# RWKV stage of a hybrid decoder step: transposes that accumulate for the sample states, row groups side by side, rank 160 cut as 80 and 80

## The chip, the cores and the metric

The kernel runs on one core of a Trainium2 chip. The metric is device time of one execution in microseconds; for the kernel before, three runs gave 1702.85, 1702.91 and 1709.01, so the median is 1702.91. One execution was profiled, and its span from first to last instruction is 1701.4 us.

## The reference

One inference step of four layers (gated DeltaNet, mLSTM, RWKV-7, gated DeltaNet), each followed by a squared-ReLU MLP, on a prompt of 256 tokens and 8 samples of one token, all sharing weights. D = 1024, so the activations are 1024 x 264 (256 + 8 columns). Everything is float32. Of the RWKV-7 layer what matters here is:

```python
xr, xw, xk, xv, xa, xg = (h + xx * mu[j] for j in range(6))
r, k, v = xr @ w_rkv[0], xk @ w_rkv[1], xv @ w_rkv[2]
w_log = -softplus(-(w0 + tanh(xw @ w1) @ w2)) - 0.5          # w1: 1024x64, w2: 64x1024
a = sigmoid(a0 + (xa @ a1) @ a2)                             # rank 64
g = sigmoid(xg @ g1) @ g2                                    # rank 160
# per sample, 16 heads of 64x64: one step of the state
s = s * w_t[:, :, None, :] + sa[..., None] * b_t[:, :, None, :] + v_t[..., None] * k_t[:, :, None, :]
```

## The kernel before, in words

Every engine has a program of its own, written by hand in order; semaphores (`wait_ge`, `then_inc`) tie them together. TensorE (PE) writes the eight banks of PSUM (`ps[0]` to `ps[7]`); ScalarE (ACT) or VectorE (DVE) copies a bank out, and `last_read[b]` holds the semaphore value that says bank b is free. A weight stream of 1 MB units goes through a ring of five slots, loaded by SyncE. A product of float32 operands that are not marked as split appears in the trace as two MATMUL records; the transposes of line 747 (`tp`, identity as the moving operand) and the split products of the MLPs appear as one each. In this document "logical" products are those written in the code.

The RWKV layer runs on PE in this order (`rwkv`, from line 1431):

1. Keys: 64 logical products `w_rkv[1]` x `xk`, k outermost (lines 1437 to 1445), all eight banks. The mixed inputs sit in two buffers: `xj[0]` holds xk, then xa, then xr; `xj[1]` holds xw, then xg, then xv. DVE (`mixed`, line 3041) may fill `xj[0]` with xa when all key products are done (line 3060), and the later ones on `lo_mm` (line 3062).
2. Down-projections (lines 1455 to 1468): four groups of 8 logical products, of 64 (w1), 64 (a1), 128 and 32 (the 160 of g1) stationary columns, into banks 3, 4, 5, 6. Then eight small transposes of the shifted row into banks 0 and 1.
3. Up-projections (`back`, line 1479): eight tiles of w2 from partitions 0 to 63 and `lo[0]`, then eight of a2 from partitions 0 to 63 and `lo[1]`. ACT takes each tile out with a sigmoid (lines 2237 to 2240).
4. `decays_to_rows` (line 1496): 16 transposes into banks 0 to 3, at once after the up-projections; then the 64 products of r with hooks between its tiles, the first of which is `cumulate_decays`; then the 64 of v.
5. Gate up-projection (line 1581 and 1632): per tile one product over 128 rows and one over 32 rows, four tiles, then four `gram` groups of 64 x 64 products, then four tiles.
6. `invert64` (line 860) inverts 64 x 64 triangular blocks in six levels. Each level has the steps (l, 0), (l, 1) and, from level 1, (l, 2), (l, 3). `PLACES` (line 554) names the steps after which a fill runs, two parts each: parts 0 to 7 are `sample_update`, 8 to 31 are `gram` and `token_major`. Sample updates sat at (0, 0), (0, 1), (1, 0), (1, 1).
7. `sample_update(q)` (line 1606) makes the new states of head pair q in bank 6 or 7: four logical products of the state (stationary, 128 x 128, already scaled by GpSimd) with the identity, which transpose it and add it in PSUM, then one product over 32 rows and 512 columns that adds the two outer products. ACT copies the bank to `rS` (line 2307), SyncE stores it.

Of the kernel before, what the change touches and what calls it, by code (L numbers as in the profile page):

```python
# [12 lines left out]
P = 128  # L13
D = 1024
# [77 lines left out]
def hybrid_trunk(nc, a, o):  # L92
# [11 lines left out]
    with ctx:  # L104
# [237 lines left out]
        rg_mm = semaphore("rg_mm")  # L342
        shT_mm = semaphore("shT_mm")
# [210 lines left out]
        PLACES = [(0, 0), (0, 1)] + [(l, i) for l in range(1, LEVELS64) for i in range(4)][:14]  # L554
# [183 lines left out]
        def _(pe):  # L738
# [692 lines left out]
            def rwkv(j):  # L1431
# [5 lines left out]
                for k in range(KT):  # L1437
                    pe.wait_ge(xj_ok, count.seen(xj_ok))
                    for t in range(KT):
# [16 lines left out]
                for i in range(4):  # L1456
                    if i == 2:
                        w = unit_in()
                    cut = (slice(0, 64), slice(64, 128), slice(0, 128), slice(128, 160))[i]
                    b = 3 + i  # L1460
                    pe.wait_ge(*last_read[b])
                    for k in range(KT):
                        if i < 3:
# [29 lines left out]
                back([(64, 0, lo[0])], w)  # L1493
                back([(64, D, lo[1])], w)

                def decays_to_rows():
                    pe.wait_ge(rk_ev, 2 * KT)
# [61 lines left out]
                def sample_reads(q0):  # L1559
# [9 lines left out]
                    if q0 == NP - 2:  # L1569
# [11 lines left out]
                back([(P, 0, lo[2]), (32, D, lo[3])], w, range(4))  # L1581
# [24 lines left out]
                def sample_update(q):  # L1606
                    b = 6 + q % 2
                    if q == 0:
                        pe.wait_ge(mvb_ok, count.seen(mvb_ok))
                        pe.wait_ge(ct_ev, count.seen(ct_ev, 2))  # L1610
                    if q % 2 == 0:
                        pe.wait_ge(qs_ok, count.seen(qs_ok))
                    pe.wait_ge(*last_read[b])
                    r_ = slice(32 * (q % 4), 32 * (q % 4) + 32)
                    for m in range(4):
                        mm(ps[b][:, m * P:(m + 1) * P], rST[:, q, m, :], ident[:], m == 0, False)
                    mm(ps[b][:], RT[r_, 1, q // 4, :], MV[q // 4][r_].rearrange("p s k -> p (s k)"), False, True).then_inc(
                        rt_mm, count.up(rt_mm))
                    last_read[b] = su_ev, count.expect(su_ev)
# [12 lines left out]
                back([(P, 0, lo[2]), (32, D, lo[3])], w, range(4, KT))  # L1632
# [3 lines left out]
                def first_fill(n):  # L1636
                    b = 6 + n % 2
                    if n < 8:
                        sample_update(n)
                    elif n < 12:  # L1640
# [198 lines left out]
        def _(ac):  # L1839
# [380 lines left out]
            def rwkv(j):  # L2220
# [9 lines left out]
                for i, (n, f) in enumerate(((64, ACT.Tanh), (64, ACT.Copy), (P, ACT.Sigmoid), (32, ACT.Sigmoid))):  # L2230
# [1358 lines left out]
```

## Time and profile before

| what | value |
|---|---|
| median of three runs | 1702.91 us |
| span of the profiled execution | 1701.4 us |
| PE busy | 1648.5 us, 97% of the span |
| DVE, ACT, POOL busy | 1029.4, 839.2, 240.6 us |
| mean granted TensorE clock | 0.994 |
| RWKV stretch that the change touches | about 767 to 985 us |

The profiled execution has no time of its own beside its span. The median of the runs is 1.5 us above the span. A timeline row gives the start, the length of the group from first start to last end, the engine, line, operation, operands, partitions x columns of the stationary operand, the form of the moving one and the count; the ends of matmuls are modelled, so the pace of a group is read from its start to the next group's start.

### The profile page before, as it was taken

Reading aid. Unit: us, or ns where it says so; the run is one execution under the profiler, and the core shown is the slowest. Engines: PE = TensorE matmul, PEld = TensorE weight load, DVE = VectorE, ACT = ScalarE, POOL = GpSimd, SP = SyncE. Lnnn points to the kernel's source line nnn. Section 1 sums busy time; section 2 is a strip of 40 time slices with the busy share of each in tenths; the row PEclk is TensorE's granted clock in tenths of the full one; section 3 lists DMA queues with packets and bytes.
Section 4 is the critical chain, followed back from the end, with each engine's and each line's share of the span. In section 5 each row is a group of like instructions: output and inputs, shape, how many; then the busy total and the mean of one; then the engine's idle time right before and its main releaser. Section 6 shows DMA issues by size and latency. Waiting matters only on the chain.

```text
span 1701.4 us, 40128 instructions
## 1 busy us (share of the span) xinstructions
PE 1648.5 (97%) x17533; PEld 1554.2 (91%) x17533; DVE 1029.4 (61%) x1688; ACT 839.2 (49%) x1599; POOL 240.6 (14%) x293
## 2 busy tenths in 40 slices
PE   7999999999998999999999999999999999999997
PEld 6999899999896999997786987999998998899997
DVE  6965677744557776435361355777448946777654
ACT  5754566633545665331522214666336745566533
POOL 6005340000010200011003130200000016310000
PEclk9999999999999999999999999999999999999999
DMA  7941345556653656544323001555557531465650
GB/s 213 273 148 38 114 146 176 190 180 199 205 160 110 213 189 197 182 138 123 127 90 112 16 4 33 147 180 188 183 174 229 175 100 40 120 195 178 198 174 26
DMA packets 244963, 250.27 MB, mean 147 GB/s; under 512 B 15936, under 2 KB 238686, under 8 KB 244702
## 3 DMA queue, kind: packets, MB, share of 16 engines
q1 hardware_dynamic: 237040, 224.74, 42.0%
q0 software_dynamic: 7440, 22.86, 4.6%
q8 instruction: 139, 2.28, 0.6%
q14 instruction: 36, 0.29, 0.1%
q10 hardware_dynamic: 308, 0.10, 0.0%
HBM read 229.75 MB, written 18.32 MB: 146 GB/s over the span
## 4 chain that ended last, share of the span: by engine, by line
PE 91%; DVE 5%; ACT 3%; issue 1%; DMA 0%; SPq 0%; DVEq 0%
PE ps L743 89%; PE ps L747 2%; DVE tri L2434 1%; DVE hn L2442 1%; ACT acts L1843 1%; DVE acts L2442 0%; DVE mixer_lo L2434 0%; ACT hn L1843 0%; DVE acts L2434 0%; DVE st L2442 0%; DVE st L2434 0%; DMA acts<-in_x_sample_dram 0%; ACT w_mlstm L1843 0%; ACT w_gdn L1843 0%; DVE acts L2438 0%
## 5 line engine op out<-in xcount | busy, mean ns | idle before, releaser
L2434 DVE TENSOR_TENSOR w_mlp<-ring,w_mlp 128x1024 fp32r<-128x1024 f32 x256 | 311.7, 1224 | 121.6 <-ACT w_mlp L1843 115.6
L1843 ACT ACTIVATE w_mlp<-ring 128x1024 fp32r<-128x1024 f32 x256 | 269.4, 1054 | 211.6 <-PE ps L743 211.6
L743 PE MATMUL ps<-hn_split,w_mlp 128*128 128x264 f32 x3072 | 373.3, 284 | 0.0
L743 PE MATMUL ps<-h_split,w_mlp 128*128 128x264 f32 x3072 | 372.6, 284 | 0.0
L743 PEld LDWEIGHTS ps<-hn_split,w_mlp 128*128 128x128 f32 x3072 | 372.0, 188 | 0.3
L743 PEld LDWEIGHTS ps<-h_split,w_mlp 128*128 128x128 f32 x3072 | 371.6, 188 | 0.0
L743 PE MATMUL ps<-gdn_hi,w_gdn 128*128 128x264 f32 x1024 | 194.9, 289 | 7.2 <-DVE mixer_lo L2434 7.0
L1843 ACT ACTIVATE tri<-ps 128x264 f32<-128x264 f32 (+4 forms) x184 | 80.9, 442 | 212.2 <-PE ps L743 211.5
L743 PEld LDWEIGHTS ps<-gdn_hi,w_gdn 128*128 128x128 f32 x1024 | 162.6, 190 | 10.8 <-issue 8.9
L1843 ACT ACTIVATE acts<-ps 128x264 f32<-128x264 f32 (+4 forms) x126 | 56.3, 451 | 205.9 <-PE ps L743 204.3
L743 PE MATMUL ps<-mixer_lo,w_gdn 128*128 128x264 f32 x512 | 146.7, 286 | 0.0
L743 PE MATMUL ps<-tri 64*64 64x64 f32 x3602 | 126.3, 221 | 3.1 <-DVE tri L2434 2.7
L743 PEld LDWEIGHTS ps<-tri 64*64 64x64 f32 x3602 | 113.3, 135 | 14.3 <-issue 12.1
L2434 DVE TENSOR_TENSOR tri<-tri 128x264 f32<-128x264 f32 (+4 forms) x145 | 59.9, 413 | 101.4 <-ACT h_split L1843 100.6
L743 PE MATMUL ps<-acts,ring 128*128 128x264 f32 (+2 forms) x448 | 105.5, 396 | 3.3 <-DVE acts L2442 2.8
L743 PEld LDWEIGHTS ps<-acts,ring 128*128 128x128 f32 (+2 forms) x448 | 83.2, 188 | 22.2 <-issue 4.9
L743 PEld LDWEIGHTS ps<-mixer_lo,w_gdn 128*128 128x128 f32 x512 | 98.1, 192 | 0.0
L2434 DVE TENSOR_TENSOR tri<-tri,ps 128x512 f32<-128x512 f32 (+1 forms) x88 | 52.5, 636 | 71.6 <-PE ps L743 71.4
L2434 DVE TENSOR_TENSOR w_gdn<-ring,w_gdn 128x1024 fp32r<-128x1024 f32 x64 | 77.9, 1218 | 21.3 <-ACT w_gdn L1843 21.3
L3444 POOL TENSOR_TENSOR hn<-hn 128x264 f32<-128x264 f32 x15 | 12.0, 797 | 510.8 <-ACT hn L1843 509.1
L2442 DVE SCALAR_TENSOR_TENSOR acts<-ps,cw,acts 128x253 f32<-128x253 f32 x144 | 69.3, 481 | 14.8 <-ACT acts L1843 11.1
L743 PE MATMUL ps<-mlstm_hi,w_mlstm 128*128 128x264 f32 x384 | 75.0, 292 | 3.1 <-DVE mixer_lo L2434 3.1
(406 smaller groups left out, 2329.3 us busy)
## 6 DMA issues: line engine op xcount, KB each, us to landing
ring<-in_ffn_w_dram SPq DMA_DIRECT2D x128, 1024.0 KB, 5.4
ring<-in_gdn_w_in_dram SPq DMA_DIRECT2D x32, 1024.0 KB, 6.2
ring<-in_ml_w_in_dram SPq DMA_DIRECT2D x12, 1024.0 KB, 5.3
ring<-in_rw_w_rkv_dram SPq DMA_DIRECT2D x12, 1024.0 KB, 5.1
st<-in_state_gdn_S_dram POOLq DMA_DIRECT2D x2, 4096.0 KB, 24.0
ring<-in_gdn_w_out_dram SPq DMA_DIRECT2D x8, 1024.0 KB, 5.0
out_gdn_S_s_dram<-st SPq DMA_DIRECT2D x16, 512.0 KB, 3.9
st<-in_state_mlstm_C_dram POOLq DMA_DIRECT2D x1, 4096.0 KB, 19.7
```

The costliest lines, as they stand in the source:

```text
L743: return nc.tensor.matmul(out, lhsT, rhs, start=start, stop=stop)
L747: return nc.tensor.transpose(out, in_, ident[0:n, 0:n])
L1843: return nc.scalar.activation(out, in_, f, bias=bias, scale=scale)
L2434: return nc.vector.tensor_tensor(out, in0, in1, op)
L2442: return nc.vector.scalar_tensor_tensor(out=out, in0=in0, scalar=s, in1=in1, op0=op0, op1=op1)
L3444: last = gp_.tensor_tensor(sq[:, 0, :], sq[:, 0, :], sq[:, k, :], ALU.add)
```

## The change

Five things are changed.

- The products of w1 and a1 now alternate: for each k one product into partitions 0 to 63 of bank 3 from `xj[1]` and one into partitions 64 to 127 of bank 4 from `xj[0]`. DVE may overwrite chunk k of `xj[0]` as soon as the key products of that chunk are done (new semaphore `xk_mm`), and starts xg when both groups are done.
- The rank-160 projection is cut as 80 and 80, down and up.
- a2 is loaded to partitions 64 to 127; the w2 and a2 tiles alternate between the two halves of the array's rows, into two banks. ACT takes them out alternately too.
- `decays_to_rows` moves from ahead of the r products to behind their first tile (hook 0.5); ACT's four copies of it move behind the load of the exponential table and the first r tile.
- The sample updates are done four at a time: 16 transposes (`is_transpose=True`, accumulating into four banks), then four products over 32 rows, one per bank and each on its own 32 partitions. They sit at (0, 0) and (0, 1); the other 24 parts sit at (l, 0), (l, 1), (l, 3) of levels 1 to 4.

```diff
-        PLACES = [(0, 0), (0, 1)] + [(l, i) for l in range(1, LEVELS64) for i in range(4)][:14]
+        PLACES = [(l, i) for l in range(1, 5) for i in (0, 1, 3)]
+        SU_BANKS = (4, 5, 6, 7, 2, 3, 4, 5)
...
-                return [([lambda r: (flatr(r)[0:64, 0:D], a["rw_w2"][0]), lambda r: (flatr(r)[0:64, D:2 * D], a["rw_a2"][0])],
+                return [([lambda r: (flatr(r)[0:64, 0:D], a["rw_w2"][0]), lambda r: (flatr(r)[64:128, 0:D], a["rw_a2"][0])],
...
-            return [([lambda r: (flatr(r)[:, 0:D], a["rw_g2"][0][0:P, :]), lambda r: (flatr(r)[0:32, D:2 * D], a["rw_g2"][0][P:, :])],
+            return [([lambda r: (flatr(r)[0:80, 0:D], a["rw_g2"][0][0:80, :]), lambda r: (flatr(r)[0:80, D:2 * D], a["rw_g2"][0][80:, :])],
...
+                        elif t == KT - 1:
+                            last.then_inc(xk_mm, count.up(xk_mm))
...
-                for i in range(4):
-                    if i == 2:
-                        w = unit_in()
-                    cut = (slice(0, 64), slice(64, 128), slice(0, 128), slice(128, 160))[i]
-                    b = 3 + i
+                for b in (3, 4):
+                    pe.wait_ge(*last_read[b])
+                count.seen(xj_ok, KT)
+                for k in range(KT):
+                    pe.wait_ge(xj_ok, count.seen(xj_ok))
+                    for i, r in enumerate(halves):
+                        last = mm(ps[3 + i][r, 0:T], w[:, k, r], xj[1 - i][:, k, :], k == 0, k == KT - 1)
+                last.then_inc(lo_mm, count.up(lo_mm, 2))
...
+                w = unit_in()
+                for i in range(2):
+                    b = 5 + i
...
-                        last = mm(ps[b][0:cut.stop - cut.start, 0:T], w[:, k, cut], xj[i != 1][:, k, :],
-                                  k == 0, k == KT - 1)
+                        last = mm(ps[b][0:80, 0:T], w[:, k, 80 * i:80 * i + 80], xj[1][:, k, :], k == 0, k == KT - 1)
...
-                back([(64, 0, lo[0])], w)
-                back([(64, D, lo[1])], w)
+                for t in range(KT):
+                    two = [(count.tiles + i) % 8 for i in range(2)]
+                    for b in two:
+                        pe.wait_ge(*last_read[b])
+                    for b, r, hid in zip(two, halves, lo):
+                        mm(ps[b][:, 0:T], w[r, t * P:(t + 1) * P], hid[r, :]).then_inc(lin_rdy, count.up(lin_rdy))
+                        last_read[b] = rk_ev, count.expect(rk_ev)
+                    count.tiles += 2
...
-                decays_to_rows()
                 linear(lambda k: xj[0][:, k, :], D, rk_ev, xj_ok,
-                       hooks={0: cumulate_decays, 1.5: lambda: sum_key_squares(0), 1: lambda: sum_key_squares(4),
+                       hooks={0.5: decays_to_rows, 0: cumulate_decays, 1.5: lambda: sum_key_squares(0), 1: lambda: sum_key_squares(4),
...
-                back([(P, 0, lo[2]), (32, D, lo[3])], w, range(4))
+                back([(80, 0, lo[2]), (80, D, lo[3])], w, range(4))
...
+                def sample_update(q0):
+                    four = [(q, SU_BANKS[q]) for q in range(q0, q0 + 4)]
...
+                    for q, b in four:
+                        if q % 2 == 0:
+                            pe.wait_ge(qs_ok, count.seen(qs_ok))
+                        pe.wait_ge(*last_read[b])
+                        for m in range(4):
+                            nc.tensor.matmul(ps[b][:, m * P:(m + 1) * P], rST[:, q, m, :], ident[:], start=m == 0, stop=False,
+                                             is_transpose=True)
+                    for q, b in four:
+                        r_ = slice(32 * (q % 4), 32 * (q % 4) + 32)
+                        mm(ps[b][:], RT[r_, 1, q // 4, :], MV[q // 4][r_].rearrange("p s k -> p (s k)"), False, True).then_inc(
+                            rt_mm, count.up(rt_mm))
+                        last_read[b] = su_ev, count.expect(su_ev)
...
-                invert64({at: lambda n=n: (first_fill(2 * n), first_fill(2 * n + 1)) for n, at in enumerate(PLACES)},
-                         RX, RM, RZ[0], RPX)
+                fills = {at: lambda n=n: (first_fill(8 + 2 * n), first_fill(9 + 2 * n)) for n, at in enumerate(PLACES)}
+                fills[0, 0], fills[0, 1] = lambda: sample_update(0), lambda: sample_update(4)
+                invert64(fills, RX, RM, RZ[0], RPX)
...
                 for n in range(KT):
                     tile(4, n, ACT.Sigmoid, V_W0)
-                for n in range(KT):
                     tile(5, n, ACT.Sigmoid, V_A0)
...
                     elif n in (0, 2):
+                        if not n:
+                            decay_rows()
                         key_squares(2 * n)
...
                     for k in range(KT):
+                        if n == 1:
+                            if k < KT - 1:
+                                dv.wait_ge(xk_mm, count.seen(xk_mm))
+                            else:
+                                dv.wait_ge(lin_rdy, base + KT)
                         mixed(into, m, k)
```

## Rows read from the trace of the kernel before

**Rows 1.** The page: shares of the chain that ended last, by engine and by line.

```profile
PE 91%; DVE 5%; ACT 3%; issue 1%; DMA 0%; SPq 0%; DVEq 0%
```

**Rows 2.** Stages: length, PE, PEld, DVE, ACT, POOL busy, PE clock, DMA share, GB/s.

```profile
767.30:798.90 31.60, 31.60 (x129) 26.27 (x129) 13.30 (x43) 2.71 (x7) 3.41 (x4) 0.91 0.27 62
798.90:813.60 14.70, 14.70 (x66) 8.94 (x66) 11.30 (x30) 1.57 (x5) 0.00 (x0) 1.00 0.94 278
901.30:915.45 14.15, 14.15 (x99) 8.29 (x98) 4.16 (x12) 3.48 (x9) 3.32 (x3) 1.00 0.22 75
935.90:984.60 48.70, 47.35 (x1410) 46.35 (x1411) 19.41 (x30) 12.54 (x21) 10.16 (x8) 1.00 0.06 14
```

**Rows 3.** Timeline of PE, keys to decays: start, length, what, count, idle before.

```profile
767.30 46.34 PE L743 MATMUL ps<-acts,ring 128*128 128x264 f32 x192 [2.77 <-DVE acts L2442]
813.57 1.04 PE L747 MATMUL ps<-ident,hn 128*9 128x128 f32 x8
814.95 7.36 PE L743 MATMUL ps<-tri,ring 64*128 64x264 f32 x32 [0.33 <-ACT acts L1843]
822.23 1.97 PE L747 MATMUL ps<-ident,acts 128*128 128x128 f32 x16
824.03 7.29 PE L743 MATMUL ps<-acts,ring 128*128 128x264 f32 x32
```

**Rows 4.** Timeline of PE around the gate's first four tiles.

```profile
901.30 5.09 PE L743 MATMUL ps<-rows,ring 128*128 128x264 f32 x16
906.32 0.44 PE L747 MATMUL ps<-ident,tri 128*128 128x128 f32 x2
```

**Rows 5.** Timeline of PE at the first sample update; seven more follow it.

```profile
916.53 1.16 PE L743 MATMUL ps<-ident,st 128*128 128x128 f32 x8
917.62 1.12 PE L743 MATMUL ps<-tri 32*128 32x512 f32 x2
918.67 1.16 PE L743 MATMUL ps<-ident,st 128*128 128x128 f32 x8
```

**Rows 6.** Timeline of ACT from the shifted rows to the first r tile.

```profile
814.22 1.06 ACT L1843 ACTIVATE acts<-ps 9x512 f32<-9x512 f32 x2 [0.16 <-PE ps L747]
815.66 7.16 ACT L1843 ACTIVATE acts<-ps,vec 128x264 f32<-128x264 f32 x16 [0.39 <-PE ps L743]
822.92 2.07 ACT L1843 ACTIVATE tri<-ps 128x512 f32<-128x512 f32 x4
825.01 1.28 ACT L1846 ACT_TABLE_LOAD   x1
```

**Rows 7.** Timeline of DVE: mixing xg after w1's products.

```profile
802.69 3.32 DVE L2442 SCALAR_TENSOR_TENSOR acts<-acts,vec,hn 128x264 f32<-128x264 f32 x8 [0.38 <-PE ps L743]
```

**Rows 8.** Timeline of PE in the first layer, where parts of the array alternate.

```profile
208.35 1.16 PE L743 MATMUL ps<-vk,tri 64*128 64x128 f32 x16
209.44 1.09 PE L743 MATMUL ps<-vk,acts 64*64 64x128 f32 x16
...
201.24 1.09 PE L743 MATMUL ps<-tri,hn 128*64 128x128 f32 x16
202.16 1.04 PE L743 MATMUL ps<-tri,acts 128*64 128x128 f32 x16
...
139.32 1.93 PE L743 MATMUL ps<-st,acts 128*16 128x128 f32 x64
141.07 0.40 PE L743 MATMUL ps<-ident,rows 128*32 128x128 f32 x8
```

**Rows 9.** Timeline of PE, levels 4 and 5 of the first inversion.

```profile
980.78 3.02 PE L743 MATMUL ps<-tri 64*64 64x64 f32 x96 [0.55 <-DVE tri L2434]
```

**Rows 10.** Timeline of POOL: the masks that the inversion starts with.

```profile
911.22 2.49 POOL L3520 TENSOR_TENSOR tri<-acts,lvl 128x512 f32<-128x512 f32 x2 [9.09 <-DVE acts L2434]
```

**Rows 11.** Timeline of PE in a run of transposes, and the stage behind it.

```profile
215.55 1.91 PE L747 MATMUL ps<-ident,tail 128*11 128x128 f32 x16
...
218.00:222.00 4.00, 3.10 (x27) 2.77 (x24) 3.69 (x6) 3.36 (x6) 0.00 (x0) 1.00 0.00 0
```

More of the change, by code:

```diff
@@ L342, in hybrid_trunk @@
         rg_mm = semaphore("rg_mm")
+        xk_mm = semaphore("xk_mm")
         shT_mm = semaphore("shT_mm")
@@ L1604, in token_major @@
                     last_read[b] = rT_ev, count.expect(rT_ev)
-                def sample_update(q):
-                    b = 6 + q % 2
-                    if q == 0:
+                def sample_update(q0):
+                    four = [(q, SU_BANKS[q]) for q in range(q0, q0 + 4)]
+                    if not q0:
                         pe.wait_ge(mvb_ok, count.seen(mvb_ok))
                         pe.wait_ge(ct_ev, count.seen(ct_ev, 2))
[L1611 to L1619, printed above, removed]
+                    for q, b in four:
[10 more added lines that the diff above has]
+                        last_read[b] = su_ev, count.expect(su_ev)
                 def bonus(q):
@@ L1631, in rwkv @@
                     gram(5, 0, c_, c_)
-                back([(P, 0, lo[2]), (32, D, lo[3])], w, range(4, KT))
+                back([(80, 0, lo[2]), (80, D, lo[3])], w, range(4, KT))
                 pe.wait_ge(ar_ok, count.seen(ar_ok))
@@ L2229, in rwkv @@
                     tile(1, n)
-                for i, (n, f) in enumerate(((64, ACT.Tanh), (64, ACT.Copy), (P, ACT.Sigmoid), (32, ACT.Sigmoid))):
+                low, high = halves
+                for i, (r, f) in enumerate(((low, ACT.Tanh), (high, ACT.Copy), (slice(0, 80), ACT.Sigmoid), (slice(0, 80), ACT.Sigmoid))):
                     ac.wait_ge(lo_mm, count.seen(lo_mm))
-                    act(lo[i][0:n, :], ps[3 + i][0:n, 0:T], f).then_inc(lo_ev, count.up(lo_ev))
+                    act(lo[i][r, :], ps[3 + i][r, 0:T], f).then_inc(lo_ev, count.up(lo_ev))
                 for h in range(2):
@@ L2238, in rwkv, with decay_rows @@
                     tile(4, n, ACT.Sigmoid, V_W0)
-                for n in range(KT):
                     tile(5, n, ACT.Sigmoid, V_A0)
-                for q in range(4):
-                    ac.wait_ge(lwT_mm, count.seen(lwT_mm))
-                    act(lwt[:, 2 * q:2 * q + 2], ps[LWT_BANKS[q]][:].rearrange("p (a c n) -> p a c n", a=2, c=2),
-                        ACT.Copy).then_inc(lwT_ev, count.up(lwT_ev))
                 exp_ln_table()
+                def decay_rows():
+                    for q in range(4):
+                        ac.wait_ge(lwT_mm, count.seen(lwT_mm))
+                        act(lwt[:, 2 * q:2 * q + 2], ps[LWT_BANKS[q]][:].rearrange("p (a c n) -> p a c n", a=2, c=2),
+                            ACT.Copy).then_inc(lwT_ev, count.up(lwT_ev))
                 def key_squares(q0):
@@ L2304, in first_fill @@
                     b = 6 + n % 2
-                    if n < 8:
-                        ac.wait_ge(rt_mm, count.seen(rt_mm))
-                        act(rS[:, n], ps[b][:].rearrange("p (s k) -> p s k", s=NS), ACT.Copy).then_inc(su_ev, count.up(su_ev))
-                    elif 12 <= n < 18:
+                    if 12 <= n < 18:
                         token_major((RV, RB, RK)[(n - 12) // 2][0], n % 2, b)
@@ L2327, in inverse_products, with sample_update @@
                                 fill[l, 2 + h]()
-                inverse_products({at: lambda n=n: (first_fill(2 * n), first_fill(2 * n + 1)) for n, at in enumerate(PLACES)})
+                def sample_update(q0):
+                    for q in range(q0, q0 + 4):
+                        ac.wait_ge(rt_mm, count.seen(rt_mm))
+                        act(rS[:, q], ps[SU_BANKS[q]][:].rearrange("p (s k) -> p s k", s=NS), ACT.Copy).then_inc(su_ev, count.up(su_ev))
+                fills = {at: lambda n=n: (first_fill(8 + 2 * n), first_fill(9 + 2 * n)) for n, at in enumerate(PLACES)}
+                fills[0, 0], fills[0, 1] = lambda: sample_update(0), lambda: sample_update(4)
+                inverse_products(fills)
                 def four(ap):
@@ L3058, in rwkv @@
                 for n, (m, into) in enumerate(((1, 1), (4, 0), (5, 1), (0, 0), (3, 1))):
[L3059 to L3062 removed]
+                    if n == 2:
+                        dv.wait_ge(lo_mm, 2)
                     elif n == 4:
@@ L3205, in first_fill @@
                         gram(RKAK[1], n - 28, b)
-                invert64({at: lambda n=n: (first_fill(2 * n), first_fill(2 * n + 1)) for n, at in enumerate(PLACES)},
+                invert64({at: lambda n=n: (first_fill(8 + 2 * n), first_fill(9 + 2 * n)) for n, at in enumerate(PLACES)},
                          RX, RM, RZ[0])
```

14 lines of the change are left out of this document (5 added, 9 removed).

## The prediction

> **What bounds the kernel now.** I read the chain of waits first: PE holds 91% of the path to the end and DMA none [rows 1]. Then the stages: in the four stages that the change touches PE is busy for all or nearly all of the time at a granted clock of 1.00, except at the start of the keys (0.91) [rows 2]. So time taken from PE here goes straight to the end, and time taken from another engine only counts where PE waits for it. The timelines say where PE waits: 2.77 us ahead of the keys and 0.33 us ahead of the up-projections [rows 3], 0.55 us in the first inversion [rows 9]. After this stretch come the MLPs, which have the same bound. So the sum is one of PE's starts, with ACT and DVE checked as followers. I count from the profiled span, 1701.4 us; the median of the runs is 1.5 us above it, and I add that back at the end.
>
> **Prices.** All are start to start. A 264-column float32 record: the four down-projections are 64 records in 813.57 - 798.9 = 14.67 us, 0.229 us each [rows 2, 3]; the up-projections are 32 in 822.23 - 814.95 = 7.28 us, 0.2275 us each [rows 3]. A logical product is two records, 0.455 us. A transpose of line 747 is one record for one logical 128 x 128: 16 in 824.03 - 822.23 = 1.80 us, 0.1125 us each [rows 3].
>
> **1. Sample updates, the large term.** One update now: eight identity records start at 916.53 and the product over 32 rows at 917.62, so four logical transposes cost 1.09 us; the product's two records cost 918.67 - 917.62 = 1.05 us; together 2.14 us, and eight make 17.1 us [rows 5]. The 0.136 us a record there, against 0.1125 for a 128-column record elsewhere, and the 1.05 us include a pause of some 0.1 us at each change between full-height products and those over 32 rows; it goes from 16 changes to 4 or so.
> After, the same transposes are one record each: 16 per group x 0.1125 = 1.80 us, plus 0.2 us for the two pauses. No row shows four row groups of 32 at work side by side. The nearest ones show other parts of the array side by side: two halves of rows into two banks, 16 records of 128 columns in 1.09 us, 0.068 us each [rows 8], where a full-height record of that size takes 0.1125 us or a bit less; and four strips of columns, 64 records of 128 columns in 141.07 - 139.32 = 1.75 us, 0.027 us each [rows 8], a quarter of 0.1125. So what is next to each other runs as many at a time as there are parts. Best case: a group of four takes one product's time, 1.05 us. Worst case: no overlap; each further product takes its records without the pauses, about 0.87 us, so 1.05 + 2.6 = 3.65 us. I take the best case, because both packed kinds in the trace reach their full factor. A group is then 1.8 + 0.2 + 1.05 = 3.05 us, two are 6.1 us: **11.0 us saved**, 5.8 us if nothing overlaps.
> If a transpose that accumulates were to cost two records as now, 32 x 0.1125 = 3.6 us would come back.
> By the Trainium skill (TensorE: Matmul & The Clock Gate, the table "Measured speedup vs the span model") four row tiles of 32 rows and 512 columns gain 3.07 times, not four; a group's four products would then take about 0.3 us more, and the estimate would save 0.6 us less. No row here shows it.
> What is behind it: ACT takes a 512-column bank in about 0.52 us (four in 2.07 us [rows 6]), four in 2.1 us, while PE is at the 64 x 64 products and the next group's transposes; banks 4 and 5 come up again only some 2 us after the first group's end. GpSimd's scaling of the states ended 9.09 us before 911.22, long before it is asked for [rows 10]. The masks for (0, 0) and (0, 1) are done at 911.22 + 2.49 = 913.7 [rows 10]; PE reached them at 915.45 [rows 2] and will now reach them 1.5 us earlier in relation, 913.95: just hidden, 0.2 us to spare.
>
> **2. Gate up-projection.** Four tiles of one full product and one over 32 rows: 16 records in 906.32 - 901.30 = 5.02 us [rows 4]; at the plain price they are 16 x 0.2275 = 3.64. The 1.4 us between are eight pauses of 0.17 us at the change of height. With 80 rows and 80 rows both products are of the full-height kind: **1.4 us saved, twice, 2.8 us**. Bounds: 0 (80 rows still pause) to 3.0. ACT has 0.9 us a tile for 0.45 us of work.
>
> **3. Down-projections.** Now 64 records, 14.67 us. The first 32 become pairs on two halves of columns. The trace has such pairs: 16 records of 128 columns in 202.16 - 201.24 = 0.92 us, 0.058 us each, half of 0.1125 [rows 8]. So 7.3 us become 3.7, with 0.1 for the first. xa must be there: chunk k is mixed while the keys run, the last 0.5 us after the keys' end, and PE asks for that one 3 us later: hidden. New wait: xg can only be mixed when both groups are done, so PE waits for a semaphore, one mix and the way back, about 0.8 us (it was hidden behind a1's products before). DVE then makes one chunk in 3.32 / 8 = 0.415 us [rows 7] against PE's 0.455: PE leads again. Then 32 records, 7.3 us: 160 columns are two products however they are cut. Sum 3.7 + 0.8 + 7.3 = 11.8 us against 14.7: **2.9 us saved**; -0.7 if the halves do not overlap (7.3 + 0.8 + 7.3), 3.7 if the wait hides.
>
> **4. Up-projections and decays.** Before: from 813.57 to the end of the first two r tiles at 831.2 is 17.6 us (1.4 to the first tile, 7.3, 1.8 of transposes, 7.1 of r) [rows 3]. After, PE could do the 16 tiles in 3.6 us, but ACT needs 7.16 us for 16 sigmoids, 0.447 each [rows 6], and eight banks is all the room there is. Let B be the start of the pairs. The first pair asks for banks 0 and 1, so for both copies of the shifted row, 0.5 us later than now: B is 1.85 us behind the shifted rows' start. ACT takes tile i out by B + 0.7 + 0.447 (i + 1); pairs 5, 6, 7 wait for it, and the last starts at B + 4.45 and ends at B + 4.9. The first r tile needs tile 8's bank, free at 4.75, and runs to B + 8.5. Then the transposes want bank 0, which holds this r tile. ACT ends its sigmoids at B + 7.9, loads its table for 1.28 us [rows 6], copies the tile out by 9.6; PE resumes at 9.75, having waited 1.3 us. Transposes to 11.55; the second r tile asks for bank 1, copied out at 11.45; it ends at B + 15.15. In all 1.85 + 15.15 = 17.0: **0.6 us saved**, where PE's own work fell by 3.6. Bounds: -1 (a further wait at the second r tile or the running sums) to 3.6. What is late next is ACT; PE's waits here are for it.
>
> **5. The fills.** The other 24 parts are the same work in other places. (4, 3) now has one; (4, 2) and (4, 3) had none, and PE waited 0.55 us for DVE behind them [rows 9]. Two parts take about 1.8 us: **0.5 us saved**. The empty places (l, 2) cost nothing: behind Q(l, 0) comes Q(l, 1), whose input ACT made one fill and 0.6 us ago. Bounds 0 to 0.6, or a loss of 0.5 at each of four levels if DVE gets behind.
>
> **Sum.** 11.0 + 2.8 + 2.9 + 0.6 + 0.5 = 17.8 us. 1701.4 - 17.8 = 1683.6 us of span, 1685.1 us for the median of the runs. Nothing downstream eats it: DMA is on 0% of the chain [rows 1], the ring's slots come free earlier by the same amount, and the state stores start earlier.
>
> **Rivals.**
> - *Row groups do not overlap* (outer products one after another, term 1): 5.2 us less, 1690.3 us. For it: not one row has 32-row groups next to each other. Against it: [rows 8]. 12%.
> - *Accumulating transposes cost two records*: 3.6 us less, 1688.7 us. They are the same instruction as line 747's apart from the flag. 5%.
> - *ACT's new place costs more*: PE's wait around the first r tile goes on into the running sums and the key squares, whose operations ACT and DVE do one after another; 3 us less, 1688.1 us. For it: ACT is the late one already. Against: 2 us of slack from the sigmoids' end to the first key square. 10%.
> - *The pairs do not do what the change says* (a2 and a1 halves run singly): terms 3 and 4 lose 3.6 + 0.6 and the new wait stays, 1689.3 us. Against: [rows 8] show both kinds. 3%.
> - *Slower: the clock.* Behind 2.77 us of idle PE [rows 3] the granted clock was down for a part of the keys (0.91 over the stage, so some 5 us at the 1.2 GHz level), and they took 31.6 us [rows 2] where 128 records x 0.2275 are 29.1, so such a fall costs 2.5 us. The two groups of updates have little ordinary work in them. If the clock falls there and stays down through the small products of the inversion, its 48.7 us [rows 2] come near to doubling: 1685 + 49 = 1734 us. It decides for "slower" once more than 18 us of PE work run at the low level. Against it: in and behind a run of transposes (16 of them from 215.55), in a stage in which PE is busy for 3.10 of 4 us, the clock is 1.00 [rows 11], and in the inversion it is 1.00 too [rows 2]. 3%.
>  The Trainium skill (TensorE: Matmul & The Clock Gate, Part 4: PE-mode transpose) says that transposes do not count as work for the clock, which is this rival's cause; the stage from 218 us does not bear it out.
> - *Something at the end of the layer eats it* (a store or load that PE meets earlier): within 0.5% of before, about 1698 us. No such wait is on PE's list. 3%.
>
> **How the numbers follow.** The forecast case has 64%: 1685.1 us, own range 1682.5 to 1688. The range of 8 in 10 takes in the first four rivals, one at a time, and the upper bounds of terms 4 and 5: 1681 to 1691. A measurement of this kernel can tell about 0.5% (8.5 us) from no change; all cases but the last two lie more than that below 1702.9: faster 0.94, same 0.03, slower 0.03.
>
> **What would show it.** Right: 32 new MATMUL records of one logical transpose each at about 0.11 us; eight 32 x 512 records per group within about 1.05 us, starting in fours; 16 up-projection tiles on PE in about 4.9 us with ACT at 7.2 us without a gap; a wait of PE for ACT of about 1.3 us behind the first r tile and for DVE of about 0.8 us ahead of the gate's down-projection; four gate tiles in 3.6 us. Wrong: 32 x 512 records one behind the other (1690); a stage with a clock under 1.00 between 800 and 970 us; a wait for GpSimd at the start of the inversion, which has only 0.2 us to spare.

## The result, and the profile after

Four runs of the changed kernel gave a median of 1688.66 us (1685.05 to 1693.14), four of the kernel before beside them 1703.14 us (1702.85 to 1709.01). The ratio is 0.9896, with an interval of 0.9876 to 0.9916: faster by 14.5 us. The span of the profiled execution fell from 1701.4 to 1686.6 us. The forecast was 1685.1 us, so the time lies in the stated range, 3.6 us above its middle. A second and a third set of runs gave 1685.99 and 1685.91 us (below).

The bound is what it was. Head of the page of the changed kernel and its shares of the chain that ended last:

```profile
span 1686.6 us, 40072 instructions
PE 1633.1 (97%) x17501; PEld 1550.6 (92%) x17501; DVE 1030.0 (61%) x1688; ACT 837.4 (50%) x1599; POOL 240.3 (14%) x293
...
PE 91%; DVE 4%; ACT 3%; issue 1%; DMA 0%; SPq 0%; DVEq 0%
```

PE's busy time fell by 15.4 us and the span by 14.8. So the time was taken out of PE's own work, and almost none of it came back as a wait. The timeline of PE of the changed kernel, from the keys to the decay sums, answers to [rows 3]:

```profile
773.46 34.12 PE L745 MATMUL ps<-acts,ring 128*128 128x264 f32 x160 [2.77 <-DVE acts L2468]
808.26 7.32 PE L745 MATMUL ps<-acts,ring 128*80 128x264 f32 x32 [0.69 <-DVE acts L2468]
815.42 1.04 PE L749 MATMUL ps<-ident,hn 128*9 128x128 f32 x8
817.26 4.66 PE L745 MATMUL ps<-tri,ring 64*128 64x264 f32 x32 [0.81 <-ACT acts L1861]
821.85 3.83 PE L745 MATMUL ps<-acts,ring 128*128 128x264 f32 x16
826.25 1.94 PE L749 MATMUL ps<-ident,acts 128*128 128x128 f32 x16 [0.57 <-ACT acts L1861]
828.05 3.83 PE L745 MATMUL ps<-acts,ring 128*128 128x264 f32 x16
831.72 3.51 PE L745 MATMUL ps<-up,tri 128*128 128x128 f32 x30
```

The reader is to see three things. The 160-column products now begin behind a wait of 0.69 us for DVE (the new wait of the down-projections). From the shifted rows to the decay sums it is 831.72 - 815.42 = 16.30 us, where it was 17.6 [rows 3]. And PE waits 0.57 us for ACT behind the first r tile, not 1.3.

The timeline of PE from the gate to the second group of updates answers to [rows 4, 5]:

```profile
901.87 3.73 PE L745 MATMUL ps<-rows,ring 80*128 80x264 f32 x16
905.43 0.38 PE L749 MATMUL ps<-ident,tri 128*128 128x128 f32 x2
...
909.38 3.83 PE L745 MATMUL ps<-rows,ring 80*128 80x264 f32 x16
913.14 1.15 PE L745 MATMUL ps<-ids,tri 64*64 64x64 f32 x32
914.22 1.97 PE L1632 MATMUL ps<-ident,st 128*128 128x128 f32 x16
916.12 1.14 PE L745 MATMUL ps<-tri 32*128 32x512 f32 x8
917.19 1.15 PE L745 MATMUL ps<-ids,tri 64*64 64x64 f32 x32
918.26 1.97 PE L1632 MATMUL ps<-ident,st 128*128 128x128 f32 x16
920.16 2.22 PE L745 MATMUL ps<-tri 32*128 32x512 f32 x40
```

Four gate tiles take 905.43 - 901.87 = 3.56 us, where it was 5.02 [rows 4]. A group of updates takes 917.19 - 914.22 = 2.97 us: 16 transposes, one record each, in 1.90 us, and four products over 32 rows in 1.07 us, as long as one took alone [rows 5]. The single records show why: of the eight, four start at 916.115, .122, .128 and .135, the other four at 916.648, .655, .662 and .668.

The windows of the changed kernel (columns as in [rows 2]) are the first 28 us of the keys, the rest to the shifted rows, the stage with the up-projections, the gate, and the two groups of updates with what lies around them:

```profile
773.46:801.46 28.00, 28.00 (x118) 23.63 (x119) 16.49 (x50) 0.61 (x2) 3.41 (x4) 0.94 0.26 58
801.46:815.42 13.96, 13.28 (x75) 8.74 (x74) 8.23 (x23) 3.66 (x10) 0.00 (x0) 1.00 0.98 290
815.42:832.00 16.58, 15.15 (x92) 11.81 (x91) 5.70 (x17) 12.55 (x30) 1.04 (x2) 1.00 0.46 148
901.87:913.14 11.27, 11.27 (x99) 9.57 (x98) 4.17 (x12) 3.40 (x9) 3.32 (x3) 1.00 0.28 95
913.14:922.21 9.07, 9.07 (x145) 7.08 (x146) 2.58 (x4) 3.29 (x7) 2.53 (x2) 1.00 0.73 195
```

The keys began at 773.46 us, where they had begun at 767.30 [rows 3], though no instruction ahead of them differs. The window ahead of the keys, of the changed kernel and then of the kernel before:

```profile
0.00:773.46 773.46, 747.19 (x7009) 713.15 (x7010) 489.38 (x797) 409.44 (x768) 124.29 (x195) 0.99 0.54 169
```

```profile
0.00:767.30 767.30, 740.67 (x7010) 706.62 (x7010) 489.24 (x797) 409.28 (x768) 124.48 (x195) 1.00 0.55 171
```

The counts agree, the granted clock reads 0.99 against 1.00. So 6.2 us of this comparison of two spans are put down to the clock. That the change itself does not slow the code ahead of it is shown by the kernel "One update after the other" below, which has all of the change but the order of a few products, and whose keys began at 767.18. The change is better read from stretches that start and end on the same instruction:

| stretch on PE, us | before | after | forecast |
|---|---|---|---|
| keys to shifted rows | 46.27 | 41.96 | -2.9 |
| shifted rows to decay sums | 17.58 | 16.30 | -0.6 |
| decay sums to gate | 70.15 | 70.15 | 0 |
| gate to first inversion | 14.15 | 11.27 | -2.8 |
| first to second inversion | 69.18 | 56.96 | -11.5 |
| keys to second inversion | 217.33 | 196.64 | -17.8 |

The first row needs one correction. The first 28 us of the keys had a lower clock in the kernel before than in the changed one (0.94, shown above). Here are the kernel before and the kernel with the updates alone changed (below), whose code up to the shifted rows is that of the kernel before:

```profile
767.30:795.30 28.00, 28.00 (x113) 23.47 (x114) 13.30 (x43) 0.00 (x0) 3.41 (x4) 0.89 0.27 60
```

```profile
768.63:796.63 28.00, 28.00 (x118) 23.65 (x119) 13.30 (x43) 0.62 (x2) 3.41 (x4) 0.94 0.27 58
```

With 0.94 the same code takes 45.03 us and not 46.27. So 1.24 us of the first row and of the last are the clock's, and the change is worth 19.45 us from the keys to the second inversion.

### The profile page after: what moved, and what is told of

It is laid out like the page before. It is cut to its first block, busy times and chain, and to the rows that moved or that the text cites. A ratio compares the mean times of both kernels' runs of the same rounds, so it can differ in the third digit from the quotient of the medians.

```text
span 1686.6 us, 40072 instructions
## 1 busy us (share of the span) xinstructions
PE 1633.1 (97%) x17501; PEld 1550.6 (92%) x17501; DVE 1030.0 (61%) x1688; ACT 837.4 (50%) x1599; POOL 240.3 (14%) x293
## 4 chain that ended last, share of the span: by engine, by line
PE 91%; DVE 4%; ACT 3%; issue 1%; DMA 0%; SPq 0%; DVEq 0%
PE ps L745 89%; PE ps L749 2%; DVE tri L2460 1%; ACT acts L1861 1%; DVE acts L2468 1%; DVE hn L2468 0%; ACT hn L1861 0%; DVE acts L2460 0%; DVE st L2468 0%; DVE st L2460 0%; DMA acts<-in_x_sample_dram 0%; ACT w_mlstm L1861 0%; ACT w_gdn L1861 0%; PE ps L1632 0%; DVE acts L2464 0%
## 5 line engine op out<-in xcount | busy, mean ns | idle before, releaser
L745 PEld LDWEIGHTS ps<-tri 64*64 64x64 f32 (+1 forms) x3602 | 111.2, 135 | 11.5 <-issue 9.4
L745 PE MATMUL ps<-tri 64*64 64x64 f32 (+1 forms) x3602 | 119.0, 221 | 2.6 <-DVE tri L2460 2.2
L745 PE MATMUL ps<-acts,ring 128*128 128x264 f32 (+2 forms) x448 | 101.0, 393 | 4.0 <-DVE acts L2468 3.5
```

Of the source, the lines that this page charges most:

```text
L745: return nc.tensor.matmul(out, lhsT, rhs, start=start, stop=stop)
```

## The experiments

In every one the stretches of this table are read from the profile and set beside those of the changed kernel.

**The change again.** The changed kernel as it is, timed with the next three on one chip.

> The changed kernel once more. The change saved 20.7 us between the start of the key products and the second inversion (217.3 us before, 196.6 us after), but the keys began 6.2 us later, in code that the change does not touch. Theory: that 6.2 us is the granted clock, which fell in other places in this one execution than in the one before (mean 0.990 against 0.994); then this execution shows its drifts at other places, the local stretch is again 196 to 197.5 us, and the median over many runs lies nearer to 18 to 20 us below before. Rival: the change itself makes the code ahead of it slower (instruction layout, loads); then the keys start again near 773.5 us and the median stays 14 to 15 us below before.

Measured: 1685.99 us (1683.85 to 1688.66, 6 runs) against 1706.64 us (1702.57 to 1712.2, 23 runs), ratio 0.9873 (0.985 to 0.9895). The stretches agree within 0.01 us but for the keys, 40.27 instead of 41.96, whose first 28 us had a clock of 1.00 instead of 0.94. The keys began at 771.82, nearer to the rival's 773.5 than to the 767.3 of before, so this run alone does not decide between the two; the 767.18 of the kernel "One update after the other" does. The change is worth more than 14.5 us, and the start of the keys wanders by itself.

**One part alone: the updates and the fills.** The diff is against the changed kernel. Gate, down- and up-projections and decays stay as before.

```diff
+                    cut = (slice(0, 64), slice(64, 128), slice(0, 128), slice(128, 160))[i]
...
-                        last = mm(ps[b][0:80, 0:T], w[:, k, 80 * i:80 * i + 80], xj[1][:, k, :], k == 0, k == KT - 1)
...
+                decays_to_rows()
...
-                back([(80, 0, lo[2]), (80, D, lo[3])], w, range(4))
+                back([(P, 0, lo[2]), (32, D, lo[3])], w, range(4))
```

> The kernel before with the sample updates alone changed (four transposes at a time, four products over 32 rows, the fills at new places). Theory of the prediction: 11.0 us from the updates and 0.5 us from the wait in level 5, so 11.5 us below before, in the stretch and in the time. Rival (the gain of a part is eaten downstream): the stretch is 11.5 us shorter, the time less than 8 us.

Measured: 1694.85 us (1690.99 to 1697.1, 6 runs), ratio 0.9921 (0.99 to 0.9942). First to second inversion 56.96, as with the whole change: the part is worth 12.2 us there, and the stretches around it are those of the kernel before.

**One part alone: the pairs, and the decays' new place.** The diffs of this part and the next are against the kernel before.

```diff
+                    for i, r in enumerate(halves):
+                        last = mm(ps[3 + i][r, 0:T], w[:, k, r], xj[1 - i][:, k, :], k == 0, k == KT - 1)
...
-                decays_to_rows()
...
+                       hooks={0.5: decays_to_rows, 0: cumulate_decays, 1.5: lambda: sum_key_squares(0), 1: lambda: sum_key_squares(4),
```

> The kernel before with w1 and a1, w2 and a2 alternating and the decays moved, and nothing else. The prediction had 2.9 + 0.6 = 3.5 us; the trace after shows 3.4 + 1.3 = 4.7 us with a wait of 0.57 us in place of 1.3 us. Theory: 4 to 5 us below before. Rival, ACT late: 3.5 us or less with a wait of over 1 us behind the first r tile.

Measured: 1703.09 us (1698.55 to 1708.3, 12 runs), ratio 0.997 (0.9956 to 0.9985). Keys to shifted rows 42.21; shifted rows to decay sums 16.30. With the clock of the keys' first 28 us at 0.94 in both, the stretch is 45.03 in the kernel with the updates alone, so the pairs are worth 2.8 us, as forecast. With the 1.3 us of the second stretch the part is worth 4.1 us, within the 4 to 5 us expected; the medians alone read 3.55.

**One part alone: 160 as 80 and 80.**

```diff
-                    cut = (slice(0, 64), slice(64, 128), slice(0, 128), slice(128, 160))[i]
+                    cut = (slice(0, 64), slice(64, 128), slice(0, 80), slice(80, 160))[i]
...
-                back([(P, 0, lo[2]), (32, D, lo[3])], w, range(4))
+                back([(80, 0, lo[2]), (80, D, lo[3])], w, range(4))
```

> The kernel before with the rank 160 cut as 80 and 80 and nothing else. Theory: the pauses at changes between full-height products and those over 32 rows are all of it, 8 per four tiles of 0.17 us, so the two groups of four tiles take 3.6 us each in place of 5.0 and 5.1 and the time is 2.8 us lower. Rival: the product over 32 rows is slow by itself and 80 rows is no cheaper than 128 plus 32; then no change.

Measured: 1703.3 us (1699.79 to 1706.19, 12 runs), ratio 0.998 (0.9965 to 0.9994). Gate to inversion 11.28, so 2.87 us less. Keys to shifted rows 44.79 against 45.03 at the same clock: the cut saves 0.24 us in the down-projections too, which the prediction had at nothing.

**All outer products on one row group.** The new sample states come from the wrong rows; only the time is read. This kernel and the next four that have no whole time beside them were run once, and only their stretches are read.

```diff
-                        r_ = slice(32 * (q % 4), 32 * (q % 4) + 32)
+                        r_ = slice(0, 32)
```

> The changed kernel, with all eight products over 32 rows taken from partitions 0 to 31 (so the sample states are not those of the reference): same count, shapes, banks and order, but the four of a group want the same rows of the array. Theory: the gain of grouping is that four row groups run at the same time; here each product waits for the one before, 0.87 us each, so a group is 2.6 us longer and first to second inversion takes 62.2 us in place of 56.95. Rival: the gain is only that PE changes less often between full height and 32 rows; then nothing changes (56.95).

Timeline of PE of this kernel, first group:

```profile
910.83 1.97 PE L1632 MATMUL ps<-ident,st 128*128 128x128 f32 x16
912.73 3.70 PE L745 MATMUL ps<-tri 32*128 32x512 f32 x8
916.35 1.76 PE L745 MATMUL ps<-ids,tri 64*64 64x64 f32 x32
918.05 2.92 PE L1632 MATMUL ps<-ident,st 128*128 128x128 f32 x16
920.90 4.78 PE L745 MATMUL ps<-tri 32*128 32x512 f32 x40
```

The four products now take 916.35 - 912.73 = 3.62 us where they took 1.07, as expected of products that queue for one row group. Behind the first they start 0.43 us apart, which for 512 columns is the pace of a full-height record (0.2225 us for 264), so 32 rows are not slow by themselves. The stretch grew by 6.68 us to 63.64, more than the 5.1 us of two groups. The rest is in the second and third line: 32 records of masks take 1.70 us instead of 1.07, and 16 transposes 2.85 instead of 1.90. Windows of this kernel:

```profile
913.00:917.00 4.00, 4.00 (x24) 1.78 (x25) 0.00 (x0) 2.33 (x4) 0.65 (x1) 0.96 0.72 207
917.00:921.00 4.00, 4.00 (x39) 3.71 (x35) 1.29 (x2) 0.06 (x1) 1.27 (x1) 0.62 0.81 181
921.00:925.00 4.00, 4.00 (x24) 1.78 (x26) 0.00 (x0) 2.16 (x4) 0.00 (x0) 1.00 0.34 76
```

The granted clock fell to its 1.2 GHz level for some 3 us behind the first group's queued products, with PE busy without a gap, at a price of 1.6 us. The second group's products queue in the same way, 3.63 us long, and behind them (921 to 925 above, and from there to 930) the clock is 1.00. So the fall came behind one of two groups in one run, and that the queued products are its cause is not shown.

**One update after the other.** Transposes in one record as in the change, but each update's product right behind them.

```diff
-                    for q, b in four:
                         r_ = slice(32 * (q % 4), 32 * (q % 4) + 32)
```

> The changed kernel, with each product over 32 rows issued right behind its own four transposes instead of behind those of all four. Theory: no product has a neighbour in another row group, so each costs 1.05 us with its pauses: 4 x (0.45 + 0.1 + 1.05) = 6.4 us a group against 2.96, first to second inversion 63.8 us in place of 56.95. Rival (order does not matter to the array, only the shapes): 57 us.

Timeline of PE of this kernel, two of the eight updates:

```profile
907.72 0.66 PE L1632 MATMUL ps<-ident,st 128*128 128x128 f32 x4
908.31 1.12 PE L745 MATMUL ps<-tri 32*128 32x512 f32 x2
909.36 0.66 PE L1632 MATMUL ps<-ident,st 128*128 128x128 f32 x4
```

An update takes 909.36 - 907.72 = 1.64 us, eight take 13.1 where the groups take 5.9. The stretch is 64.12, 7.17 us longer. Being on different rows is not enough; the products have to be next to each other. The keys of this kernel:

```profile
767.18 3.26 PE L745 MATMUL ps<-acts,ring 128*128 128x264 f32 x7 [2.77 <-DVE acts L2467]
```

They begin as early as in the kernel before (767.30), ahead of them the granted clock was 1.00 again.

**Identity products instead of accumulating transposes.**

```diff
-                            nc.tensor.matmul(ps[b][:, m * P:(m + 1) * P], rST[:, q, m, :], ident[:], start=m == 0, stop=False,
-                                             is_transpose=True)
+                            mm(ps[b][:, m * P:(m + 1) * P], rST[:, q, m, :], ident[:], m == 0, False)
```

> The changed kernel, grouped as it is, with plain products by the identity in place of the accumulating transposes. Theory: 32 logical products of two records in place of one, 32 x 0.1115 = 3.6 us more, first to second inversion 60.5 us. Rival: the transpose in an accumulation costs the same as two records, no change.

Timeline of PE of this kernel, the first group:

```profile
915.17 3.84 PE L745 MATMUL ps<-ident,st 128*128 128x128 f32 x32
918.94 1.14 PE L745 MATMUL ps<-tri 32*128 32x512 f32 x8
```

32 records in 3.77 us instead of 16 in 1.90, twice: 3.74 us on the stretch (60.70). The products behind them are untouched.

**The decays ahead of r again, all else as changed.**

```diff
+                decays_to_rows()
...
-                       hooks={0.5: decays_to_rows, 0: cumulate_decays, 1.5: lambda: sum_key_squares(0), 1: lambda: sum_key_squares(4),
+                       hooks={0: cumulate_decays, 1.5: lambda: sum_key_squares(0), 1: lambda: sum_key_squares(4),
```

> The changed kernel, with the decays' transposes back ahead of the r products and ACT's copies of them ahead of its table load. From the start of the up-projections to the running sums it was 16.2 us before and is 14.45 us in the changed kernel. Theory: ACT's 16 sigmoids (6.0 us when it does not wait) set the end of the up-projections, and the move hides what is left of them behind an r tile; without it PE waits for the last decay tile, so 4.6 + about 2.3 of waiting + 1.8 + 7.1 = 15.8 to 16.3 us. Rival: packing the rows alone gives the 1.3 us and the move gives nothing: 14.5 us.

Timeline of PE of this kernel:

```profile
815.30 4.65 PE L745 MATMUL ps<-tri,ring 64*128 64x264 f32 x32 [0.81 <-ACT acts L1862]
821.75 1.96 PE L749 MATMUL ps<-ident,acts 128*128 128x128 f32 x16 [1.79 <-ACT acts L1862]
```

PE waits 1.79 us for ACT. Up-projections to decay sums are 15.37 us; 16.21 before, 14.45 with the change. So of the 1.76 us on this stretch the packed tiles bring 0.84 and the new place 0.92. The 15.37 lie below the 15.8 to 16.3 expected, which let the transposes wait for the last of 16 sigmoids. They wait for the fifteenth (`rk_ev` of 3 * KT - 1, the eight tiles of the keys counted in; the last sigmoid is one of a2's). It ends at 821.69 in this trace, 6.4 us behind the start of the pairs, where 6.9 were assumed.

**The fills in the places that follow each other.** 24 parts at every step of levels 1 to 3.

```diff
-        PLACES = [(l, i) for l in range(1, 5) for i in (0, 1, 3)]
+        PLACES = [(l, i) for l in range(1, 4) for i in range(4)]
```

> The changed kernel, with its 12 fills at (l, 0) to (l, 3) of levels 1 to 3 instead of (l, 0), (l, 1), (l, 3) of levels 1 to 4. Theory: PE waits 0.55 us for DVE in level 5 and again for as much in level 4, where each step now has nothing behind it: first to second inversion 57.5 to 58.5 us in place of 56.95. Rival: the place of the fills does not matter: 56.95.

Timeline of PE of this kernel:

```profile
964.87 3.02 PE L745 MATMUL ps<-tri 64*64 64x64 f32 x96 [0.54 <-DVE tri L2460]
```

The wait of [rows 9] is back with its 0.54 us. In the changed kernel PE goes on there without a gap up to the wait that ends the stretch in both:

```profile
965.36 3.90 PE L745 MATMUL ps<-tri 64*64 64x64 f32 x128
970.10 1.15 PE L745 MATMUL ps<-ids,tri 64*64 64x64 f32 x32 [0.84 <-DVE tri L2460]
```

The stretch is 57.97, 1.02 us longer. The 0.54 us understate the wait, since idle time is counted from the modelled end of the record ahead. That record starts at 964.11 and the next at 964.87, 0.76 us later, where such records start 0.03 us apart on average; so the wait costs 0.73 us. Two pauses too short for a row of their own, 0.15 us at 931.9 and 0.09 us at 936.0, are most of the rest. The second wait that the expectation names, in level 4, is not there.

**A further version.** The changed kernel with its three waits between the down-projections and the decay sums taken away (0.69, 0.81 and 0.57 us): xg is mixed chunk by chunk behind its own pair, the shifted rows go into banks 2 and 7, the decays into banks 2 to 5.

```diff
-        LWT_BANKS, CUM_BANKS = (0, 1, 2, 3), (0, 1, 2, 3)
+        LWT_BANKS, CUM_BANKS, SH_BANKS = (2, 3, 4, 5), (0, 1, 2, 3), (2, 7)
...
+                    if k < KT - 1:
+                        last.then_inc(xk_mm, count.up(xk_mm))
...
+                        elif n == 2:
+                            if k < KT - 1:
+                                dv.wait_ge(xk_mm, count.seen(xk_mm))
+                            else:
+                                dv.wait_ge(lo_mm, 2)
```

> The changed kernel without the three waits that its trace shows PE in between the down-projections and the running sums: xg chunk by chunk behind the pairs of w1 and a1 (0.69 us), the shifted rows' transposes in banks 2 and 7, which the up-projections ask for later (0.81 us), the decays' transposes in banks 2 to 5, so that they do not wait for the first r tile's copy (0.57 us). Theory: PE is the bound and ACT starts its sigmoids 0.8 us earlier, so keys to shifted rows is 0.7 us shorter and shifted rows to running sums 16.3 - 1.4 = 14.9 us; 2 us in all, 0.1% of the time, seen in the stretch and hardly in the median. Rival: ACT's 16 sigmoids and table load still set the end, so only 0.7 to 1.2 us come.

Timeline of PE of this kernel:

```profile
772.04 39.71 PE L745 MATMUL ps<-acts,ring 128*128 128x264 f32 x192 [2.77 <-DVE acts L2470]
811.59 1.04 PE L749 MATMUL ps<-ident,hn 128*9 128x128 f32 x8
812.55 4.69 PE L745 MATMUL ps<-tri,ring 64*128 64x264 f32 x32
817.17 3.83 PE L745 MATMUL ps<-acts,ring 128*128 128x264 f32 x16
820.83 1.91 PE L749 MATMUL ps<-ident,acts 128*128 128x128 f32 x16
```

All three waits are gone. Keys to shifted rows are 39.54 us, 0.73 less than with the change at the same clock; shifted rows to up-projections 0.88 less, from there to the decay sums 0.86 less. Time: 1683.63 us (1682.95 to 1687.33, 4 runs) against 1706.68 us (1701.65 to 1713.31, 11 runs), ratio 0.9867 (0.9846 to 0.9888).

**The change a third time,** beside that version on one chip.

> The changed kernel a third time, on the same chip as the one without its waits. Theory: the stretch from the up-projections to the second inversion is the same to 0.05 us (14.45, 70.15, 11.27, 56.95), the time of the keys moves with the clock, and the ratio to before is again 0.987 to 0.989. Rival: the first comparison, 0.9896, was the right one and the second, 0.9873, the odd one.

Measured: 1685.91 us (1681.65 to 1690.32, 6 runs), ratio 0.9878 (0.9856 to 0.99). The further version's median is 2.3 us below it, and the stretches say 2.47. The whole times of the two alone would not settle it, since their intervals overlap; the rows do.

**Whole times and the clock.** A line fitted by least squares through all runs of the kernels that were run more than once (84 runs with a clock on record; one constant for each kernel, one slope on the mean granted clock) gives 1.13 us for each 0.001 of clock and leaves a scatter of 1.3 us. At equal clock the changed kernel comes out 19.4, 20.4 and 19.9 us below the kernel before in its three sets, the three parts 12.95, 3.6 and 3.3 us (19.9 together), and the further version 22.2. The stretches say the same: 19.45 us for the change, and for its parts 12.2, 4.1 and 3.1 us.

## Why the prediction was right

- **The bound.** Right. PE had 91% of the chain and kept it, and the stage between, decay sums to gate, did not move by 0.01 us.
- **Term 1, the updates: 11.0 us.** Right, by 0.2. Both groups are 2.97 us, forecast 3.05. Both causes were shown apart: without neighbouring row groups 3.62 instead of 1.07 us a group, without the transpose form 3.77 instead of 1.90. The factor from the halves and strips of [rows 8] carried over to four row groups. By the Trainium skill (TensorE: Matmul & The Clock Gate, the table "Measured speedup vs the span model") it would be 3.07; here 3.62 / 1.07 = 3.4, with 0.19 us of pauses in both times, and 3.9 without them, so the row lies above the page's figure and the estimate of 0.6 us less is not borne out.
- **Term 2, the gate: 2.8 us.** Right: 2.87, and with it the reason, since products of 80 rows do not pause. The single records give the pause a finer shape than "eight of 0.17 us": in the kernel before they start at 901.305, .528, .844, 902.170, .481 and .808, so behind the first pair 0.31 to 0.33 us apart, in the changed one 0.22 to 0.23. At each change of height there is some 0.1 us ahead of the first record and 0.1 us behind it, seven times 0.2 us.
- **Term 3, the down-projections: 2.9 us.** Right for the pairs (2.8), the new wait 0.69 for 0.8. The cut at 80 gave 0.24 us beside it, which the sum had at nothing ("160 columns are two products however they are cut"): together 3.07 us at equal clock.
- **Term 4, up-projections and decays: 0.6 us.** Too small by half; 1.3 us measured. The step of this term that failed is "ACT needs 7.16 us for 16 sigmoids, 0.447 each". The row read for it [rows 6] has 16 sigmoids at 7.16 us with no wait noted, but that was the pace at which PE delivered the tiles (0.455). With tiles in pairs PE makes one in 0.22 us, and ACT shows its own pace. Timeline of ACT of the changed kernel:

```profile
816.06 1.06 ACT L1861 ACTIVATE acts<-ps 9x512 f32<-9x512 f32 x2
817.98 6.04 ACT L1861 ACTIVATE acts<-ps,vec 128x264 f32<-128x264 f32 x16 [0.86 <-PE ps L745]
824.04 1.28 ACT L1864 ACT_TABLE_LOAD   x1
825.71 0.39 ACT L1861 ACTIVATE acts<-ps 128x264 f32<-128x264 f32 x1 [0.39 <-PE ps L745]
```

 6.04 / 16 = 0.378 us each, or 0.363 from start to start. Sixteen of them end 1.1 us earlier than forecast, so PE's wait behind the first r tile was 0.57 us, not 1.3. Put into the prediction's own steps, with B the start of the pairs: they end at about B + 4.3, the first r tile at 7.95, ACT has its table by then (0.7 + 6.05 + 1.28 = 8.03) and copies the tile out by 8.45, PE resumes at 8.6, and the second r tile ends at 14.05. In all 15.9 us, where 17.0 were forecast and 16.3 measured; most of the 0.4 us between is the end of the pairs, which came at B + 4.6. What is late now is no more the sigmoids but the r tile's own way through ACT. The start of the pairs, 1.85 us behind the shifted rows, came out at 1.84.
- **Term 5, the fills: 0.5 us.** The wait is gone, and it comes back when the fills are moved. Its size was read too small: the 0.55 us of [rows 9] are idle time from a modelled end, while the records on its two sides start at 980.02 and 980.78, 0.76 us apart where 0.03 is usual, so it cost 0.73 us. The whole stretch gave 12.2 us where terms 1 and 5 had 11.5. Of the 0.7 us more, 0.2 are the groups (17.1 to 5.9 us is 11.2) and 0.2 this wait. The 0.3 us left lie in the 64 x 64 records: in the kernel before the updates break into them at four places and in the changed one at two, and at each place the record that follows an update takes 0.10 us and the one ahead of the next 0.15 us, where 0.03 is usual, so 0.19 us a place and some 0.4 us for two. This is read from single records of the two traces; no run isolates it.
- **"Just hidden, 0.2 us to spare".** Right. GpSimd's masks in the changed kernel:

```profile
910.27 2.49 POOL L3549 TENSOR_TENSOR tri<-acts,lvl 128x512 f32<-128x512 f32 x2 [7.57 <-DVE acts L2460]
```

 They are done at 912.76, and PE starts on them at 913.14, 0.4 us later.
- **The rivals.** Row groups without overlap, double-priced transposes and single pairs are each refuted by a run or a row. The clock held at 1.00 through both groups and 16 + 16 transposes (window 913.14 to 922.21). By the Trainium skill (TensorE: Matmul & The Clock Gate, Part 4: PE-mode transpose) transposes are no work for the clock; in these two groups that had no effect, with products between them. Whether longer runs of them would show it, no run here says.
- **The whole time.** 17.8 us were forecast from the sum; at equal clock it was 19.4 to 20.4. The sum was 1.65 us too small: 0.7 us in the stretch of terms 1 and 5, 0.7 us in term 4, 0.2 us in term 3 and 0.1 us in term 2. The first comparison read 14.5; its two profiles differ ahead of the keys by four more stretches of 3.4 us at the 1.2 GHz level, some 1.5 us each, and the fit gives the set as a whole 19.4 at equal clock. So the first median lay near the forecast in part by luck, by two errors of opposite sign: some 2 us too little in the sum and about 5 us from the clock. The 1685.99 and 1685.91 of the later sets owe their nearness to luck as well: the forecast counted down from 1702.91, while the kernel before, with more runs, has a median of 1706.6, and that makes up for what the sum lacks. What was right is the mechanism, term by term in the stretches.

## What to carry to other kernels

An engine's own pace is read only from a row in which nothing is delivered to it in between: the same sixteen sigmoids took 0.447 us each when PE made the tiles one by one and 0.378 when PE was ahead. An idle time in a row is counted from a modelled end, so what a wait costs is read from the starts of the records on its two sides: 0.76 us here where the row said 0.55. Products over a part of the array's rows are worth ordering so that neighbours use different parts and different banks, and a width such as 160 is better cut into equal parts than into 128 and a rest, since each change of height cost some 0.2 us here. Where whole times wander with the clock by more than the change is worth, compare a stretch between two instructions that both kernels have.

## What the runs showed of the hardware that was not expected

- Eight 32-row records on one row group, 3.62 us with PE busy all the time, were followed once by some 3 us at the 1.2 GHz level (granted clock 0.62 from 917 to 921 us), though PE was busy throughout; behind the second such group of the same run the clock was 1.00, as it was behind both groups spread over four row groups (1.07 us each). What decides between the two is not shown.
- Unchanged code of 767 us took 6.2 us longer in one profile than in another at a granted clock of 0.99 instead of 1.00, in four steps of some 1.5 us. The kernel before alone ranged from 1701.65 to 1713.31 us.
- A 32-row float32 record of 512 columns starts 0.43 us behind the one before it when both want the same rows, and four on different rows start within 0.02 us of each other; at a change between full height and 32 rows some 0.1 us is lost on either side of the first record.
